# Prompt attention of a two-layer decoder step: scores from split operands in place of a plain f32 product

## The chip, the cores and the metric

The kernel runs on one core of a Trainium2 chip, in one launch. The metric is device time in microseconds, the median of three runs. The core has a matrix engine (TensorE, PE in the rows; its weight loads are PEld), a vector engine (VectorE, DVE), a scalar engine (ScalarE, ACT), GpSimd (POOL) and SyncE (SP), which here only issues transfers. ScalarE issues transfers too.

## The reference, cut to what matters

One inference step of a decoder of two layers: a Conformer convolution layer, then a layer of forgetting attention, each followed by a SwiGLU feed-forward. A prompt of 1024 tokens and eight sample requests of four tokens each go through it together. D is 1024, with 16 heads of 64. In the attention layer, for the prompt:

```python
p = xn @ w_in                     # q, k, v and the forget gate in one projection
logf = log_sigmoid(p[..., 3*D:] + b_f)
c = cumsum(logf, axis=1)
s = einsum('bqhd,bkhd->bhqk', qi, k) * dh**-0.5
s = s + ci[:, :, :, None] - cT[:, :, None, :]
s = where(kpos[None, :] <= qpos[:, None], s, -inf)
pr = softmax(s, axis=-1)
o = einsum('bhqk,bkhd->bqhd', pr, v)
```

Keys, values and logf of the prompt and of the samples are outputs as well. The samples attend to a paged cache of 1024 past rows each. All inputs and outputs are f32.

## The kernel before, in words

Activations are kept with features on the 128 partitions and the 1056 tokens (1024 prompt, 32 sample) along the free dimension, in three blocks of 352 columns. All large products are made of three passes over rounded operands (fp32r): each operand is split into a rounded part and the difference, as in xhi and xlo, whi and wlo, and `unit_block` (L693 to L709) adds up hi by hi, lo by hi and hi by lo. A unit is one chunk of 128 output features: three blocks by eight chunks by three passes, 72 matmuls. Weights are loaded by SP two units ahead, rounded by ScalarE (`hi_part`, L1133), and the difference is taken by GpSimd (`low_parts`, L618). Each engine has its own program; semaphores are the only order between them, and each engine and each transfer queue works in the order in which it is written.

In the attention layer the projection runs over pairs of units q: four pairs of queries (from Q_ATTN_IN), then the forget gate (L843 to L856), four pairs of keys (from QK), and four pairs of values (from QV). For queries and keys VectorE moves each block from PSUM to the staging tile stg, with one slot for each half s of a pair (`qk_half`, L1678), and ScalarE stores the 1024 prompt columns of it to q_scr or k_scr in device memory (`store_staged`, L1286). Keys and values are also transposed to token rows on TensorE (`keys_tr`, L858) and moved out by ScalarE (`keys_out`, `values_out`). The negated sums of logf, negct, are stored to c_scr (L1362). The sums for the sample requests are made by TensorE from the cached logf (L922 to L929), copied by VectorE to cbT (L1750) and stored by ScalarE to cb_scr (L1373).

Then comes the prompt attention, with heads in pairs. SP loads a head's queries, keys and its row of negated sums into one of two slots s of qa and ka (`load_head`, L505); the sums are the 65th row of ka, and the 65th row of qa is set to ones (L1756), so that one f32 product of 65 rows gives the scores with the sums of the keys. (The sum of the query's row falls out of the softmax.) A slot is loaded again when the last scores from it are through. Each head has eight query tiles of 128 rows, in the order 3, 2, 1, 0, 7, 6, 5, 4; tile qt has (qt + 1) * 128 key columns, done in pieces of up to 512. For tile t (`prompt_pair`, L978, L1383, L1777): TensorE makes the scores; VectorE adds the mask on the diagonal block (L1784) and takes the maximum (L1786); ScalarE makes the exponents and their sum (L1394); TensorE transposes them (`probs_tr`, L943); ScalarE copies them to pt (L1381); TensorE multiplies by the values (`values`, L952); VectorE divides (`output`, L1760). On TensorE the scores of tile t stand before the transposes of tile t-1 and the values of tile t-2; on ScalarE the copy of t-1 stands before the exponents of t.

After that come the eight sample requests, whose key pages SP loads into four buffers (`load_k`, L519). The first four pages are issued while the prompt attention runs (L543), the others after its last values (L546).

## Time and profile before

| | us |
|---|---|
| runs | 3438.42, 3446.14, 3453.70 |
| median | 3446.14 |
| span of the profiled execution | 3441.0 |
| TensorE busy | 2972.1 (86%) |
| VectorE busy | 1332.7 (39%) |
| ScalarE busy | 994.2 (29%) |
| GpSimd busy | 971.2 (28%) |

For the profiled execution the profile gives the span, from its first to its last instruction; its own time with what lies around the span is not listed apart from the runs. Matmuls are pipelined, so that their records overlap and a record is longer than the step from one start to the next; a plain f32 matmul shows as two weight loads and two matmuls. The granted clock of TensorE (PEclk) has two levels, 1.00 for 2.4 GHz and 0.50 for 1.2 GHz; a figure between them is a mean over a stretch. A wait is shown with the engine and the line that ended it; "issue" means that nothing in the profile ended it.

The projection of queries, keys and values takes the span from about 1500 to 1812 us, the prompt attention from 1824 to 2213, the sample requests from there to about 2500.

### The profile page before, as it was taken

The numbers are of one execution on the slowest core, as the hardware profiler recorded it, in microseconds if no ns is written. First come the engines' busy times: TensorE is split into PE (matmuls) and PEld (weight loads), VectorE is DVE, ScalarE is ACT, GpSimd is POOL, SyncE is SP. The second block draws the span as 40 slices with busy tenths as digits, with TensorE's granted clock in tenths as the row PEclk, the third lists the DMA queues.
The fourth block names the chain that finished last, engine by engine and source line by source line (L and its number), as shares of the span: only waits on it lengthen the run. The fifth ranks groups of instructions, "written<-read, shape, count | busy, mean of one in ns | idle before, by whom it ended". The sixth has DMA issues, their size and how long they took to land.

```text
span 3441.0 us, 49665 instructions
## 1 busy us (share of the span) xinstructions
PE 2972.1 (86%) x17970; PEld 2775.7 (81%) x17970; DVE 1332.7 (39%) x2005; ACT 994.2 (29%) x1549; POOL 971.2 (28%) x436
## 2 busy tenths in 40 slices
PE   5535336999999999989999999899898999999998
PEld 4535335889999999979997777778797999999997
DVE  6999996421111111251113555555334111111114
ACT  4323225232111111221113544455423211111113
POOL 2757571222212121231110000055613122222221
PEclk9767667999999999999996999988789999999998
DMA  3000000111111111122411201377511111111111
GB/s 95 19 24 12 24 12 20 43 37 40 52 40 46 43 43 49 37 68 82 121 39 31 70 25 25 101 254 262 195 43 37 40 46 43 40 52 34 52 36 70
DMA packets 243747, 206.54 MB, mean 60 GB/s; under 512 B 18252, under 2 KB 218956, under 8 KB 243652
## 3 DMA queue, kind: packets, MB, share of 16 engines
q1 hardware_dynamic: 230535, 186.66, 17.8%
q10 hardware_dynamic: 13133, 18.80, 1.6%
q8 instruction: 52, 0.85, 0.1%
q14 instruction: 27, 0.22, 0.0%
HBM read 183.16 MB, written 23.13 MB: 60 GB/s over the span
## 4 chain that ended last, share of the span: by engine, by line
PE 72%; DVE 15%; issue 7%; ACT 3%; DMA 1%; POOL 1%; DVEq 0%; ACTq 0%; SPq 0%; POOLq 0%
PE PS L706 19%; PE PS L708 18%; PE PS L707 18%; DVE yacc L1644 8%; PE PS L964 4%; PE PS L990 3%; PE PS L948 2%; DVE tm L1506 2%; PE PS L1027 1%; DVE rs L1485 1%; PE PS L1068 1%; PE PS L1040 1%; PE PS L1069 1%; PE PS L1041 1%; ACT pr L1394 1%
## 5 line engine op out<-in xcount | busy, mean ns | idle before, releaser
L706 PE MATMUL PS<-xhi,whi 128*128 128x352 f32 x3456 | 1144.4, 331 | 269.0 <-DVE u L1608 188.3
L708 PE MATMUL PS<-xlo,whi 128*128 128x352 f32 x3456 | 1122.3, 325 | 0.0
L707 PE MATMUL PS<-xhi,wlo 128*128 128x352 f32 x3456 | 1121.0, 324 | 0.0
L622 POOL TENSOR_TENSOR wlo<-wraw,whi 128x1024 fp32r<-128x1024 f32 x208 | 510.7, 2456 | 1608.4 <-ACT whi L1136 1608.4
L706 PEld LDWEIGHTS PS<-xhi,whi 128*128 128x128 f32 x3456 | 657.5, 190 | 311.6 <-DVE u L1608 190.3
L707 PEld LDWEIGHTS PS<-xhi,wlo 128*128 128x128 f32 x3456 | 660.9, 191 | 0.0
L708 PEld LDWEIGHTS PS<-xlo,whi 128*128 128x128 f32 x3456 | 658.6, 191 | 0.0
L1543 DVE TENSOR_TENSOR ht<-PS,ht 128x352 f32<-128x352 f32 x132 | 69.1, 525 | 908.4 <-PE PS L708 904.4
L1136 ACT ACTIVATE whi<-wraw 128x1024 fp32r<-128x1024 f32 x208 | 218.8, 1052 | 595.2 <-PE PS L708 567.2
L706 PE MATMUL PS<-hhi,whi 128*128 128x352 f32 x1056 | 341.2, 323 | 8.8 <-issue 8.8
L707 PE MATMUL PS<-hhi,wlo 128*128 128x352 f32 x1056 | 338.5, 321 | 0.0
L708 PE MATMUL PS<-hlo,whi 128*128 128x352 f32 x1056 | 338.2, 320 | 0.0
L1644 DVE SCALAR_TENSOR_TENSOR yacc<-u,wc,yacc 128x1024 f32<-128x1024 f32 x152 | 329.5, 2168 | 3.7
L679 POOL TENSOR_TENSOR Vl<-vr,Vh 128x1024 fp32r<-128x1024 f32 x64 | 151.7, 2383 | 531.6 <-ACT Vh L1420 531.6
L1529 DVE TENSOR_TENSOR X<-PS,X 128x352 f32 x216 | 113.3, 525 | 446.8 <-PE PS L708 446.4
L644 POOL TENSOR_TENSOR yp<-yp,prods 128x1024 f32<-128x1024 f32 x72 | 217.0, 3013 | 10.3
L706 PEld LDWEIGHTS PS<-hhi,whi 128*128 128x128 f32 x1056 | 198.1, 188 | 10.8 <-issue 10.8
L707 PEld LDWEIGHTS PS<-hhi,wlo 128*128 128x128 f32 x1056 | 198.4, 188 | 0.0
L708 PEld LDWEIGHTS PS<-hlo,whi 128*128 128x128 f32 x1056 | 197.9, 187 | 0.0
L1241 ACT ACTIVATE prods<-u,wc 128x1024 f32<-128x1024 f32 x88 | 98.7, 1148 | 298.7 <-DVE u L1613 199.3
L1191 ACT ACTIVATE hhi<-ht 128x352 f32 x132 | 65.5, 498 | 410.6 <-DVE ht L1543 410.6
L990 PE MATMUL PS<-ka,qa 65*128 65x512 f32 (+3 forms) x384 | 165.6, 544 | 3.6 <-issue 3.6
(197 smaller groups left out, 3036.5 us busy)
## 6 DMA issues: line engine op xcount, KB each, us to landing
wraw<-in_ffn_w_gu SPq DMA_DIRECT2D x88, 512.0 KB, 3.8
kr<-in_cache_k SPq DMA_DIRECT2D x64, 512.0 KB, 4.8
vr<-in_cache_v SPq DMA_DIRECT2D x64, 512.0 KB, 4.8
wraw<-in_ffn_w_down SPq DMA_DIRECT2D x32, 384.0 KB, 3.4
wraw<-in_attn_w_in SPq DMA_DIRECT2D x24, 512.0 KB, 3.9
wraw<-in_ffn_w_down SPq DMA_DIRECT2D x32, 320.0 KB, 3.1
wraw<-in_conv_w_in SPq DMA_DIRECT2D x16, 512.0 KB, 3.8
wraw<-in_conv_w_out SPq DMA_DIRECT2D x8, 512.0 KB, 4.0
```

The source lines that it names most:

```text
L622: nc.gpsimd.tensor_tensor(wlo[:, s, :], wraw[:, s, :], whi[:, s, :].bitcast(F32), ALU.subtract).then_inc(w_lo, 1)
L644: nc.gpsimd.tensor_tensor(yp[:, :], prods[:, 0, :] if i == 1 else yp[:, :], prods[:, i % 3, :], ALU.add).then_inc(p_tap, 1)
L679: nc.gpsimd.tensor_tensor(Vl[:, j % 2, :], raw_values(j), Vh[:, j % 2, :].bitcast(F32), ALU.subtract).then_inc(v_lo, 1)
L706: nc.tensor.matmul(out, wh, hi[:, k, blk(b)], start=(k == 0), stop=False)
L707: nc.tensor.matmul(out, wl, hi[:, k, blk(b)], start=False, stop=False)
L708: m = nc.tensor.matmul(out, wh, lo[:, k, blk(b)], start=False, stop=(k == kc - 1))
L964: m = nc.tensor.matmul(PS[:, 6 + t % 2, 0:DH], pt[:, t % 2, kb * P:(kb + 1) * P], v, start=(kb == 0), stop=(kb == nb - 1))
L990: m = nc.tensor.matmul(PS[:, 2 * (t % 2) + k0 // 512, 0:k1 - k0], qa[:, s, qt * P:(qt + 1) * P], ka[:, s, k0:k1], start=True, stop=True)
L1136: nc.scalar.activation(whi[:, s, :], wraw[:, s, :], ACT.Copy).then_inc(w_hi, 1)
L1241: nc.scalar.activation(prods[:, i % 3, :], u[:, k:k + SEQ], ACT.Copy, scale=wc[:, R_DW + k:R_DW + k + 1]).then_inc(a_tap, 1)
L1529: nc.vector.tensor_tensor(xs, PS[:, NB * s + b, 0:BW], xs, ALU.add).then_inc(ev[s], 1)
L1644: step(nc.vector.scalar_tensor_tensor(yacc[:, :], u[:, k:k + SEQ], wc[:, R_DW + k:R_DW + k + 1], yacc[:, :], ALU.mult, ALU.add))
```

## The change

Queries and keys are split into a rounded part (hi) and the difference (lo) right after the projection: ScalarE copies each staged block to shi, rounded; VectorE subtracts it into slo; ScalarE stores both, to two scratch tensors each. The negated sums are split in the same way (chi, clo). A head now loads q1 = (q hi over q hi) and k1 = (k hi over k lo), each of 128 rows, and q2 = (q lo and two rows of ones) and k2 = (k hi and the two rows of the sums), each of 66 rows. The scores are two matmuls on rounded operands that add up in PSUM: q1 by k1, and q2 by k2. The product of the two lo parts is left out.

The new tiles lie where others lay: shi and slo in the place of Vt (values), q2 in the place of cbT, pt in the place of ktok, two of the buffers of the key pages. From this come new waits: SP loads heads after cbT has been stored, VectorE sets the ones after that too, values are written after the last stores of queries and keys, and key pages 2 and 3 of the first request are loaded after the last values of the prompt.

```diff
--- before.py
+++ after.py
@@ -190,10 +190,19 @@
         lc = at("lc", [P, NPG, NREQ, H], F32, where["sq"][0])
         cbT = at("cbT", [NREQ * H, NPG * P], F32, where["rs"][0])
 
-        qa = at("qa", [DH + 1, 2, SEQ], F32, where["xhi"][0])
-        ka = at("ka", [DH + 1, 2, SEQ], F32, after("qa"))
-        pr = at("pr", [P, 2, SEQ], F32, after("ka"))
-        pt = at("pt", [P, 2, SEQ], F32, after("pr"))
+        shi = at("shi", [P, 2, SEQ], FR, where["Vt"][0])
+        slo = at("slo", [P, 2, SEQ], FR, after("shi"))
+        chi = at("chi", [H, SEQ], FR, where["rs"][0])
+        clo = at("clo", [H, SEQ], FR, where["ssq"][0])
+
+        q1 = at("q1", [P, 2, SEQ], FR, where["xhi"][0])
+        k1 = at("k1", [P, 2, SEQ], FR, after("q1"))
+        k2 = at("k2", [DH + 2, 2, SEQ], FR, after("k1"))
+        pr = at("pr", [P, 2, SEQ], F32, after("k2"))
+        assert after("pr") <= where["xlo"][0]
+        q2 = at("q2", [DH + 2, 2, SEQ], FR, where["rs"][0])
+        assert after("q2") <= where["tm"][0]
+        pt = at("pt", [P, 2, SEQ], F32, where["ktok"][0])
         on = at("on", [P, NT, P], F32, where["tm"][0])
         OT = at("OT", [P, C, T], F32, where["xlo"][0])
 
@@ -224,9 +233,9 @@
         yn = at("yn", [P, C, T], F32, where["xhi"][0])
         ytok = at("ytok", [P, 2, D], F32, H0)
 
-        q_scr = nc.dram_tensor("q_scr", (D, SEQ), F32).ap()
-        k_scr = nc.dram_tensor("k_scr", (D, SEQ), F32).ap()
-        c_scr = nc.dram_tensor("c_scr", (H, SEQ), F32).ap()
+        q_scr = [nc.dram_tensor(f"q_scr{part}", (D, SEQ), F32).ap() for part in ("hi", "lo")]
+        k_scr = [nc.dram_tensor(f"k_scr{part}", (D, SEQ), F32).ap() for part in ("hi", "lo")]
+        c_scr = nc.dram_tensor("c_scr", (2, H, SEQ), F32).ap()
         cb_scr = nc.dram_tensor("cb_scr", (NREQ * H, NPG * P), F32).ap()
 
         PS = ctx.enter_context(nc.psum_tensor("PS", [P, 8, 512], F32))
@@ -290,6 +299,10 @@
         c_neg = sem("c_neg")
         c_tr = sem("c_tr")
         c_nc = sem("c_nc")
+        c_hi = sem("c_hi")
+        c_lo = sem("c_lo")
+        st_hi = sem("st_hi")
+        st_lo = sem("st_lo")
         c_st = sem("c_st")
         lc_ld = sem("lc_ld")
         x_mm = sem("x_mm")
@@ -499,14 +512,23 @@
             for s in range(2):
                 sp.wait_ge(mm[s], Q_ATTN_OUT * NB)
             for s in range(2):
-                sp.wait_ge(stg_st[s], 16 * C)
-            sp.wait_ge(c_st, 16)
+                sp.wait_ge(stg_st[s], 32 * C)
+            sp.wait_ge(c_st, 32)
+
+            sp.wait_ge(x_ev, 2)
+            sp.wait_ge(cb_st, 16)
 
             def load_head(i, s):
                 h = i * 2 + s
-                sp.dma_start(qa[0:DH, s, :], q_scr[ds(h * DH, DH), :]).then_inc(a_ld[s], 16)
-                sp.dma_start(ka[0:DH, s, :], k_scr[ds(h * DH, DH), :]).then_inc(a_ld[s], 16)
-                sp.dma_start(ka[DH:DH + 1, s, :], c_scr[ds(h, 1), :]).then_inc(a_ld[s], 16)
+                rows = ds(h * DH, DH)
+                sp.dma_start(q1[0:DH, s, :].bitcast(F32), q_scr[0][rows, :]).then_inc(a_ld[s], 16)
+                sp.dma_start(k1[0:DH, s, :].bitcast(F32), k_scr[0][rows, :]).then_inc(a_ld[s], 16)
+                sp.dma_start(q1[DH:P, s, :].bitcast(F32), q_scr[0][rows, :]).then_inc(a_ld[s], 16)
+                sp.dma_start(k1[DH:P, s, :].bitcast(F32), k_scr[1][rows, :]).then_inc(a_ld[s], 16)
+                sp.dma_start(q2[0:DH, s, :].bitcast(F32), q_scr[1][rows, :]).then_inc(a_ld[s], 16)
+                sp.dma_start(k2[0:DH, s, :].bitcast(F32), k_scr[0][rows, :]).then_inc(a_ld[s], 16)
+                sp.dma_start(k2[DH:DH + 2, s, :].bitcast(F32), c_scr[:, ds(h, 1), :].rearrange("a h t -> a (h t)")
+                             ).then_inc(a_ld[s], 16)
             load_head(0, 0)
             load_head(0, 1)
             with sp.Fori(1, C) as i:
@@ -540,14 +562,13 @@
 
             for s in range(2):
                 sp.wait_ge(kt_st[s], 16 * C // 2)
-            for j in range(4):
+            for j in range(2):
                 load_k(0, j)
 
             sp.wait_ge(a_pv, NTILES)
             sp.wait_ge(w_lo, 2 * Q_ATTN_OUT + 2)
-            sp.wait_ge(cb_st, 16)
             load_sums(0)
-            for j in range(4, NPG):
+            for j in range(2, NPG):
                 load_k(0, j)
 
             def load_step(b):
@@ -981,15 +1002,16 @@
                 for t in range(NTAU):
                     s, qt = t // NT, ORDER[t % NT]
                     if t % NT == 0:
-                        pe.wait_ge(a_ld[s], i * 48 + 48)
+                        pe.wait_ge(a_ld[s], i * 112 + 112)
 
                     past(pe, a_exp, base + (t - 1))
                     nk = (qt + 1) * P
-                    for k0 in range(0, nk, 512):
-                        k1 = min(nk, k0 + 512)
-                        m = nc.tensor.matmul(PS[:, 2 * (t % 2) + k0 // 512, 0:k1 - k0],
-                                             qa[:, s, qt * P:(qt + 1) * P], ka[:, s, k0:k1],
-                                             start=True, stop=True)
+                    for e0 in range(0, nk, 512):
+                        e1 = min(nk, e0 + 512)
+                        out = PS[:, 2 * (t % 2) + e0 // 512, 0:e1 - e0]
+                        nc.tensor.matmul(out, q1[:, s, qt * P:(qt + 1) * P], k1[:, s, e0:e1], start=True, stop=False)
+                        m = nc.tensor.matmul(out, q2[:, s, qt * P:(qt + 1) * P], k2[:, s, e0:e1],
+                                             start=False, stop=True)
                     m.then_inc(a_sc, 1)
                     if t >= 1:
                         probs_tr(base, t - 1)
@@ -1285,10 +1307,18 @@
 
             def store_staged(q, s, scr, q0):
 
-                act.wait_ge(ev[s], seen(s, q, NB - 1))
-                act.nop(nofuse=True)
-                act.dma_start(scr[ds(q * (2 * P) + (s * P - q0 * 2 * P), P), :], stg[:, s, 0:SEQ]
-                              ).then_inc(stg_st[s], 16)
+                past(act, stg_st[s], (q - Q_ATTN_IN) * 32)
+                for b in range(NB):
+                    act.wait_ge(ev[s], seen(s, q, b))
+                    act.nop(nofuse=True)
+                    cols = slice(b * BW, min((b + 1) * BW, SEQ))
+                    nc.scalar.activation(shi[:, s, cols], stg[:, s, cols], ACT.Copy).then_inc(st_hi, 1)
+                act.wait_ge(st_hi, (q - Q_ATTN_IN) * (2 * NB) + (s * NB + NB))
+                act.wait_ge(st_lo, (q - Q_ATTN_IN) * (2 * NB) + (s * NB + NB))
+                for part, split in zip(scr, (shi, slo)):
+                    act.nop(nofuse=True)
+                    act.dma_start(part[ds(q * (2 * P) + (s * P - q0 * 2 * P), P), :], split[:, s, :].bitcast(F32)
+                                  ).then_inc(stg_st[s], 16)
 
             with act.Fori(Q_ATTN_IN, QK) as q:
                 for s in range(2):
@@ -1359,14 +1389,21 @@
             next_hi(QV, 0)
             next_hi(QV, 1)
             act.wait_ge(c_nc, 2)
-            act.dma_start(c_scr, negct[:, :]).then_inc(c_st, 16)
+            nc.scalar.activation(chi[:, :], negct[:, :], ACT.Copy).then_inc(c_hi, 1)
+            for s in range(2):
+                act.wait_ge(stg_st[s], 32 * C)
             values_out(QV, 0)
+            act.wait_ge(c_hi, 1)
+            act.wait_ge(c_lo, 1)
+            act.dma_start(c_scr[0], chi[:, :].bitcast(F32)).then_inc(c_st, 16)
+            act.dma_start(c_scr[1], clo[:, :].bitcast(F32)).then_inc(c_st, 16)
             with act.Fori(QV + 1, Q_ATTN_OUT) as q:
                 next_hi(q, 0)
                 values_out(q - 1, 1)
                 next_hi(q, 1)
                 values_out(q, 0)
             values_out(Q_ATTN_OUT - 1, 1)
+            act.wait_ge(c_st, 32)
             new_out(vnew, 2)
             act.wait_ge(kt_ev, 4 * C)
             act.wait_ge(x_ev, 2)
@@ -1393,6 +1430,8 @@
                     past(act, a_tr, base + (t - 1))
                     nc.scalar.activation(pr[:, t % 2, 0:nk], banks(2 * (t % 2), nk), ACT.Exp,
                                          bias=nmx[:, t:t + 1], accum_out=den[:, t:t + 1]).then_inc(a_exp, 1)
+            for s in range(2):
+                act.wait_ge(kt_st[s], 16 * C // 2)
             prompt_pair(0)
             act.dma_start(v_prompt[0, 0].rearrange("(t p) h d -> p t (h d)", p=P), Vt[:, :, :]).then_inc(v_st, 16)
             act.dma_start(v_sample[0].rearrange("b t h d -> (b t) (h d)"), vnew[:, :]).then_inc(v_st, 16)
@@ -1679,10 +1718,6 @@
 
                 u = (q - Q_ATTN_IN) * 2 + s
 
-                if values:
-                    dve.wait_ge(stg_st[s], 16 * C)
-                else:
-                    past(dve, stg_st[s], (q - Q_ATTN_IN) * 16)
                 if keys:
                     past(dve, kt_tr, ((q - QK) * 2 + (s - 1)) * 2)
                 for b in range(NB):
@@ -1693,6 +1728,11 @@
                             PS[:, NB * s + b, BW - NS:BW], scale, None, ALU.mult).then_inc(nqk, 1)
                     nc.vector.tensor_scalar(stg[:, s, blk(b)], PS[:, NB * s + b, 0:BW], scale, None,
                                             ALU.mult).then_inc(ev[s], 1)
+                for b in range(0 if values else NB):
+                    dve.wait_ge(st_hi, u * NB + (b + 1))
+                    cols = slice(b * BW, min((b + 1) * BW, SEQ))
+                    nc.vector.tensor_tensor(slo[:, s, cols], stg[:, s, cols], shi[:, s, cols].bitcast(F32),
+                                            ALU.subtract).then_inc(st_lo, 1)
 
             def qk_pair(q, scale, keys, values=False):
                 for s in range(2):
@@ -1743,9 +1783,13 @@
                 dve.wait_ge(c_tr, half + 1)
                 nc.vector.tensor_copy(negct[:, 512 * half:512 * half + 512], PS[0:H, 6 + half, :]
                                       ).then_inc(c_nc, 1)
+            dve.wait_ge(c_nc, 2)
+            dve.wait_ge(c_hi, 1)
+            nc.vector.tensor_tensor(clo[:, :], negct[:, :], chi[:, :].bitcast(F32), ALU.subtract).then_inc(c_lo, 1)
             with dve.Fori(QV + 1, Q_ATTN_OUT) as q:
                 qk_pair(q, 1.0, True, True)
             dve.wait_ge(x_mm, 1)
+            dve.wait_ge(c_st, 32)
             for half in range(2):
                 nc.vector.tensor_copy(cbT[:, 512 * half:512 * half + 512], PS[:, 6 + half, :]).then_inc(x_ev, 1)
             dve.wait_ge(nm_tr, 1)
@@ -1753,7 +1797,8 @@
                                   ).then_inc(x_ev, 1)
 
 
-            nc.vector.memset(qa[DH:DH + 1, :, :], 1.0).then_inc(a_ones, 1)
+            dve.wait_ge(cb_st, 16)
+            nc.vector.memset(q2[DH:DH + 2, :, :].bitcast(F32), 1.0).then_inc(a_ones, 1)
 
             dve.wait_ge(out_st, 16 * 3)
```

## Rows read from the trace of the kernel before

**Rows 1.** The page: its first line and the chain's shares by line.

```profile
span 3441.0 us, 49665 instructions
...
PE PS L706 19%; PE PS L708 18%; PE PS L707 18%; DVE yacc L1644 8%; PE PS L964 4%; PE PS L990 3%; PE PS L948 2%; DVE tm L1506 2%; PE PS L1027 1%; DVE rs L1485 1%; PE PS L1068 1%; PE PS L1040 1%; PE PS L1069 1%; PE PS L1041 1%; ACT pr L1394 1%
```

**Rows 2.** Chain that ended last, attention stretch: start us, us, engine and line.

```profile
1835.39 3.52 PE PS L990 x4
...
1873.79 3.52 PE PS L990 x4
...
2012.28 1.79 PE PS L990 x4
...
2057.26 1.79 PE PS L990 x4
```

**Rows 3.** Timeline of one head: start us, us, engine, line, operation [idle before].

```profile
2012.60 0.19 PEld L990 LDWEIGHTS PS<-ka,qa 65*128 65x128 f32 x1 [0.24 <-issue]
...
2013.03 0.19 PEld L990 LDWEIGHTS PS<-ka,qa 65*128 65x128 f32 x1 [0.24 <-issue]
...
2016.94 1.09 PE L948 MATMUL PS<-ident,pr 128*128 128x128 f32 x8 [0.82 <-ACT pr L1394]
...
2020.14 0.98 PE L948 MATMUL PS<-ident,pr 128*128 128x128 f32 x7 [0.59 <-ACT pr L1394]
```

**Rows 4.** Waits of TensorE, 1824 to 2213: total us, times, longest.

```profile
PE PS L948 <- ACT pr L1394: 21.1, 31, 0.8
```

**Rows 5.** Timeline of TensorE, sample stage, rounded operands of 512 columns.

```profile
2299.81 0.39 PE L1068 MATMUL PS<-Vh,PTs 128*128 128x512 f32 x1
2300.04 0.39 PE L1069 MATMUL PS<-Vl,PTs 128*128 128x512 f32 x1
```

**Rows 6.** Groups by line: count, busy us, mean ns, idle before.

```profile
L1147 ACT ACTIVATE xhi<-tm 128x352 fp32r<-128x352 f32 x96 | 47.8, 498 | 78.6 <-DVE tm L1506 78.6
```

**Rows 7.** Timelines of ScalarE and TensorE at the forget gate.

```profile
1584.05 1.06 ACT L1136 ACTIVATE whi<-wraw 128x1024 fp32r<-128x1024 f32 x1 [10.30 <-PE PS L708]
...
1587.73 0.66 PE L847 MATMUL PS<-xhi,wfs 128*128 128x352 f32 x1 [3.71 <-DVE wfs L1707]
```

**Rows 8.** Timeline of TensorE at the end of the keys.

```profile
1702.75 1.03 PE L887 MATMUL PS<-ident,newqk 128*32 128x128 f32 x8 [1.49 <-ACT ktok L1316]
```

**Rows 9.** Timelines at the start and the end of prompt attention.

```profile
1821.79 0.36 ACTq L1373 DMA_DIRECT2D cb_scr<-cbT  x1
...
1824.35 3.32 PE L990 MATMUL PS<-ka,qa 65*128 65x512 f32 x4 [3.62 <-issue]
...
2210.96 0.63 SPq L536 DMA_DIRECT2D cbx<-cb_scr  x1
```

**Rows 10.** DMA issues: size and us from issue to landing.

```profile
cb_scr<-cbT ACTq DMA_DIRECT2D x1, 512.0 KB, 2.6
```

**Rows 11.** DMA queues, 1806 to 1830: packets, MB, share of that time.

```profile
q1 hardware_dynamic: 324, 1.06, 20.4%
```

**Rows 12.** Windows: length, busy us of PE, PEld, DVE, ACT, POOL, then PEclk.

```profile
1824.00:1884.00 60.00, 58.53 (x187) 42.96 (x188) 19.97 (x53) 17.10 (x39) 0.00 (x0) 0.50 0.04 9
1885.00:2208.00 323.00, 299.90 (x1969) 234.19 (x1968) 178.03 (x470) 162.33 (x345) 0.00 (x0) 1.00 0.14 41
...
2126.50:2130.00 3.50, 2.75 (x11) 1.27 (x9) 2.56 (x6) 1.46 (x3) 0.00 (x0) 1.00 0.00 0
2208.50:2212.00 3.50, 2.05 (x17) 1.62 (x15) 1.39 (x5) 0.00 (x0) 0.00 (x0) 1.00 0.00 0
...
2213.60:2220.40 6.80, 6.04 (x29) 5.53 (x28) 3.14 (x3) 3.69 (x4) 0.00 (x0) 0.50 0.44 125
...
2273.50:2276.50 3.00, 3.00 (x19) 2.47 (x18) 2.29 (x4) 2.75 (x4) 2.13 (x1) 0.50 0.34 132
2277.00:2280.00 3.00, 2.37 (x17) 1.96 (x16) 2.14 (x5) 1.97 (x2) 2.07 (x1) 1.00 0.35 108
```

**Rows 13.** Timeline of TensorE, 2270 to 2278.

```profile
2275.45 1.75 PE L1027 MATMUL PS<-ident,kr 128*128 128x128 f32 x8
```

## The prediction

> **What bounds the kernel now.** I read the page's chain of waits first, then the attention stretch by its chain in order of time, its timeline and its waits, then windows for the clock. The chain runs through the projection and feed-forward matmuls (L706 to L708), which the diff leaves alone; of what it touches, L990 (scores) holds 3% of a 3441.0 us span, L964 4%, L948 2% [rows 1]. The prompt attention is 16 heads of 8 query tiles. In its steady part two heads take 44.98 us (2012.28 to 2057.26) [rows 2], 22.5 a head.
>
> Inside a head TensorE does, per tile, scores, the transposes of the tile before and the values of the one before that. A plain f32 score matmul of 512 columns is two records, 0.43 us apart by the starts of their weight loads [rows 3], so 0.86. Tiles are 512, 384, 256, 128, 1024, 896, 768 and 640 columns wide: 4608 columns, nine times 512, 7.7 us a head. But TensorE is not the bound at every tile: before the transposes of the 1024 and the 896 tile it stands for 0.82 and 0.59 us until ScalarE's exponent is through [rows 3], and over the stage such waits come to 21.1 us [rows 4]. From one of these transposes to the next is 3.2 us (2016.94 to 2020.14), a ring of transposes, ScalarE's copy, its exponent and again transposes, with no score matmul in it.
>
> **The matmuls.** Rounded operands of 512 columns start 0.23 us apart [rows 5]; two passes make 0.46 instead of 0.86. Nine such: 4.1 instead of 7.7, 3.6 less a head, 58 over 16. How much arrives, tile by tile (0.78 us per 1000 columns): the 1024 tile saves 0.80, and since the long wait behind it starts at its end, all of it counts. The 896 tile lies inside that wait, the 768 tile beside the 3.2 us ring: nothing, the waits grow by 0.70 and 0.60. The 640, 512, 384, 256 and 128 tiles save 0.50, 0.40, 0.30, 0.20 and 0.10, 1.5 together, where the trace shows TensorE itself late; ScalarE's ring comes next there, and I take 1.1. So 1.9 a head, 30 us. The bounds are 0.8 (13 us) and 3.6 (58 us) a head. That 128 columns go as fast, each, as 512 is not shown; if the two 128 wide pieces of a head gained nothing, 0.2 a head, 3 us, would go. Contraction rows (128 and 66 for 65) are not in the time of a matmul; I cost them at nothing.
>
> **Splitting at the projection.** 16 units of queries and keys each gain three ScalarE copies (0.5 us each, as the same shape takes in L1147 [rows 6]), three VectorE differences of about that, and a second store. ScalarE stands 10.30 us before its next piece of a unit [rows 7], which hides these 2.4 us (with the last difference and the second issue); VectorE no longer waits for the store of the unit. Without that cover it would be 16 times 2.4, 38 us. It shows at two places where TensorE already waits for these engines. At the forget gate it waits 3.71 us for VectorE's wfs [rows 7], which waits for a ScalarE copy now queued behind three copies, the last difference and one more issue: 1.5 + 0.5 + 0.4, 2.4, and 3 with some of it at the low clock (2 to 5). At the end of the keys it waits 1.49 us for ScalarE's ktok [rows 8], behind the same three things: 2.4 again, I take 3 (2 to 5). The split of the sums c lies beside four pairs of value projections, nobody waits for it before the loads: nothing.
>
> **The start of attention.** In the kernel before, SP issues the loads of the first two heads ahead of time, beside the last projection work. The change makes SP wait until cbT is stored, because q2 lies in its place; behind that wait on SP stand all head loads. The store is issued at 1821.79 [rows 9] and lands 2.6 us later [rows 10], 1824.4. A head is now six transfers of 256 KB and one of 8, 1.58 MB instead of 0.52. Two heads' old loads, 1.06 MB, took 20.4% of 24 us [rows 11], 4.9 us or 216 GB/s; so 7.3 us, plus 1.4 for the first issue and the wake-up (an estimate, half of the 2.6): scores start near 1833.1 and not at 1824.35 [rows 9]. That is 9 us. The bounds are 5, at twice that rate, and 16.5, with both heads' 3.2 MB mixed. VectorE's memset of the ones (now two rows) waits for the same store and lies beside the loads. Later loads, 7.3 us a head in 20, hide; nothing else is on SP's queue then.
>
> **The end of attention.** pt takes the place of two page buffers, so key pages 2 and 3 of the first request are loaded after the last values, behind SP's load of the sums at 2210.96 [rows 9]; TensorE has pages 0 and 1 to transpose first: 1.5 us (0 to 3, as a transfer of that size lands in 2.6 [rows 10]).
>
> **The clock.** From 1824 to 1884 the granted clock was 0.50, the level of 1.2 GHz, after TensorE had stood for 3.62 us [rows 9, 12]; a head cost 38.4 us there (1835.39 to 1873.79) [rows 2] instead of 22.5. With the change a head there saves nine times 0.80, some 7 us, less a little for waits: 32. But the full clock is nearer its end later on. It held over 2126.5 to 2130.0 with TensorE busy 2.75 of 3.50 us, and was 0.50 after 2208.5 to 2212.0, busy 2.05 of 3.50 [rows 12]; halving the scores of the first of these stretches takes 0.7 us out of it. I expect a low stretch at the start about as long as now, cheaper by some 7, and about one new fall inside the stage, dearer by about the same: 0. Bounds: 20 less (no low stretch), or 140 more (all heads low).
> The Trainium skill ("TensorE: Matmul & The Clock Gate", PE-mode transpose) says that transposes don't engage the full clock. By that rule the change takes away half of what holds it, and the all-low rival below would be the time. The trace speaks against it: 2273.5 to 2276.5 was at 0.50 with transposes on TensorE, and 2277 to 2280 is at 1.00 [rows 12, 13].
> The same page (Why this matters for your kernels) asks for no idle gaps over about 3 us; by that rule the grown waits, at most 1.5 us, would cost no clock at all. No run here shows it yet: the fall behind 2208.5 came with 1.45 us idle in all.
>
> **Sum.** Against the profiled execution (span 3441.0): -30 + 9 + 3 + 3 + 1.5 + 0 = -13.5. The median of the runs, 3446.14, lies 5.1 above that span; 13 off it gives 3433.
>
> **Rivals.**
> Scores alone set the pace: TensorE's 58 us arrive, or the low stretch at the start goes (20): 41 or 33 less, 3405 to 3413. For it, TensorE is busy 299.90 of 323 us of the stage [rows 12]; against it, the waits on ScalarE of [rows 3, 4].
> Costs eat the gain: of the five smaller tiles nothing arrives (13 us for 30), or less than half of it while the loads of two heads mix (16.5 for 9) and the two projection waits run to 5: 3446 to 3461. For it, ScalarE's ring, which already ends some tiles; against it, that these five show no wait as long as at the two wide ones [rows 3].
> The low clock comes back in attention, the one that ends slower: place, the waits before the transposes of the 1024 and 896 tiles, now 1.5 and 1.2 us; price, 32 less 20.6, 11.4 us a head at 1.2 GHz. It decides from about 1.2 heads more than now (gain gone); from 2.7 heads more, the result is slower by over 0.5%. All 16 low: 16 times 32 is 512 instead of 387 (1824.35 to 2210.96) [rows 9], plus 16.5 of other costs, on the median: 3588. For it, the two stretches above; against it, the full clock from 1885 to 2208 [rows 12] in spite of the same two waits in every head.
> The change doesn't do what it says: a rounded pass on 128 rows takes as long as an f32 record (0.43); then no gain and 16.5 more, 3463. Against it, [rows 5].
>
> **Chances.** Forecast 0.50 (own range 3420 to 3448), pace 0.17, costs 0.15, clock 0.13, no speed-up 0.05. A measurement of this kernel can tell about 0.5%, 17 us, from no change. Faster than 3429: the pace and two fifths of the forecast, 0.37; slower than 3463: clock, most of the no speed-up, 0.18; same 0.45. The range 3406 to 3468 leaves out the all-low end of the clock and the best of the pace, under 0.2.
>
> **What would show it.** In the profile after: pairs of score records 0.23 apart at 512 columns; a head near 20.6; waits before the 1024 and 896 transposes of about 1.5 and 1.2; first scores 9 us later behind the cbT store; L847 and the new-key transposes 2 to 3 later behind ScalarE. I am wrong if heads take under 19.5 or over 22, if windows inside attention after the first two heads show a clock well under 1.00 for long, or if the first scores start within 6 us of the old place.

## The result, and the profile after

The changed kernel took 3474.58 us (median of four runs, 3459.56 to 3480.02) where the kernel before took 3449.44 beside it (3438.42 to 3453.70): ratio 1.0079, interval 1.0049 to 1.0110. That is slower by 0.8%, where 3433 and a gain of 0.4% were forecast, and above the range of 3406 to 3468. Here and below the ratios rest on the runs in the faster of the core's two states, so they are not the quotients of the medians, which are over all runs. The profiled execution took 3459.56 us and is the fastest of the four; its span, 3457.8, is 16.8 us longer than the 3441.0 of [rows 1].

The page of the changed kernel: span, granted clock in 40 slices, the chain's shares by line. L1012 and L1013 are the two score passes, L969 the transposes, L985 the values.

```profile
span 3457.8 us, 50031 instructions
...
PEclk9767667999999999999996798989789999999999
...
PE PS L727 19%; PE PS L729 18%; PE PS L728 18%; DVE yacc L1683 8%; PE PS L985 4%; PE PS L969 2%; DVE tm L1545 2%; PE PS L1049 1%; DVE rs L1524 1%; PE PS L1090 1%; PE PS L1012 1%; PE PS L1091 1%; PE PS L1062 1%; PE PS L1063 1%; PE PS L1013 1%
```

Scores fell from 3% of the chain to about 2%, as meant; the time went elsewhere. Three marks cut the span, here from the timelines of ScalarE's, SP's and TensorE's queues in the changed kernel (start us, us, what [idle before]):

```profile
1830.45 0.36 ACTq L1410 DMA_DIRECT2D cb_scr<-cbT  x1
...
1833.14 0.56 SPq L524 DMA_DIRECT2D q<-q_scrhi  x1
...
1843.10 0.77 PE L1012 MATMUL PS<-k,q 128*128 128x512 f32 x1 [13.70 <-DMA k<-c_scr]
...
2230.91 0.65 SPq L558 DMA_DIRECT2D cbx<-cb_scr  x1
```

Against [rows 9] the store of cbT is 8.7 us later (the projection), the first scores 18.75 later (so 10.1 more at the start of attention). From first scores to the load of the sums it is 387.8 us where it was 386.6: the stage that should have lost 30 us lost nothing. What follows it is 3.1 shorter.

The pace of the heads was as forecast. Starts of the 16 value matmuls of the 1024 tile, from the chain in order of time:

```profile
1865.09 3.31 PE PS L985 x16
1897.31 3.31 PE PS L985 x16
...
2002.20 1.73 PE PS L985 x16
2023.67 1.73 PE PS L985 x16
2043.51 1.73 PE PS L985 x16
```

Two heads take 41.31 us from 2002.20, 20.65 each (forecast 20.6); at the start one takes 32.2 (forecast 32). One head from TensorE's timeline, the counterpart of [rows 3], and the waits from 1843 to 2213, the counterpart of [rows 4] (up to the stage's end at 2230.9 they come to 37.5 us in 35 waits):

```profile
2015.74 0.40 PE L1013 MATMUL PS<-k,q 66*128 66x512 f32 x1
2015.98 0.40 PE L1012 MATMUL PS<-k,q 128*128 128x512 f32 x1
...
2019.49 1.10 PE L969 MATMUL PS<-ident,pr 128*128 128x128 f32 x8 [1.50 <-ACT pr L1431]
...
2022.69 0.98 PE L969 MATMUL PS<-ident,pr 128*128 128x128 f32 x7 [1.17 <-ACT pr L1431]
```

```profile
PE PS L969 <- ACT pr L1431: 34.7, 32, 2.7
```

The passes start 0.24 apart and the two waits grew to 1.50 and 1.17, where 1.5 and 1.2 were forecast. What was not foreseen stands in the windows (length, busy us of PE, PEld, DVE, ACT, POOL, then PEclk):

```profile
1833.20:1918.40 85.20, 70.31 (x294) 64.80 (x295) 29.06 (x74) 26.42 (x57) 0.00 (x0) 0.50 0.43 124
1918.50:1966.20 47.70, 39.77 (x302) 35.64 (x301) 29.32 (x77) 24.96 (x54) 0.00 (x0) 1.00 0.31 70
1966.30:2000.30 34.00, 33.27 (x141) 30.81 (x139) 12.34 (x34) 12.25 (x26) 0.00 (x0) 0.50 0.21 47
2000.40:2102.70 102.30, 87.77 (x677) 79.63 (x677) 61.49 (x164) 55.42 (x119) 0.00 (x0) 1.00 0.34 77
2102.80:2136.80 34.00, 33.27 (x141) 30.81 (x140) 12.34 (x34) 12.15 (x26) 0.00 (x0) 0.50 0.20 47
2136.90:2230.90 94.00, 80.44 (x625) 73.19 (x623) 53.40 (x143) 50.23 (x105) 0.00 (x0) 1.00 0.26 62
```

153.2 us ran at 1.2 GHz (0.50) in three stretches. The first began while TensorE still waited for the loads, so 143.3 us of them lie after the first scores; the kernel before had one stretch of about 60 there [rows 12]. An estimate from the heads' own times: at 32 us a head, 143.3 us are 4.5 heads that cost 11.4 more each, 51; the stretch before was 1.6 heads of 38.4 that cost 15.9 more each, 25. The difference, 26, is most of the 30 us that the shorter score work saved.

### The profile page after: what moved, and what is told of

It is laid out like the page before. It is cut to its first block, busy times and chain, and to the rows that moved or that the text cites. A ratio compares the mean times of both kernels' runs of the same rounds, so it can differ in the third digit from the quotient of the medians.

```text
span 3457.8 us, 50031 instructions
## 1 busy us (share of the span) xinstructions
PE 2958.0 (86%) x17970; PEld 2813.3 (81%) x17970; DVE 1368.2 (40%) x2054; ACT 1014.3 (29%) x1598; POOL 972.1 (28%) x436
## 4 chain that ended last, share of the span: by engine, by line
PE 71%; DVE 15%; issue 8%; ACT 3%; DMA 1%; POOL 1%; DVEq 0%; SPq 0%; ACTq 0%; POOLq 0%
PE PS L727 19%; PE PS L729 18%; PE PS L728 18%; DVE yacc L1683 8%; PE PS L985 4%; PE PS L969 2%; DVE tm L1545 2%; PE PS L1049 1%; DVE rs L1524 1%; PE PS L1090 1%; PE PS L1012 1%; PE PS L1091 1%; PE PS L1062 1%; PE PS L1063 1%; PE PS L1013 1%
## 5 line engine op out<-in xcount | busy, mean ns | idle before, releaser
L727 PE MATMUL PS<-hhi,whi 128*128 128x352 f32 x1056 | 341.2, 323 | 8.8 <-issue 8.8
L985 PEld LDWEIGHTS PS<-Vt,pt 128*128 128x128 f32 x1152 | 170.7, 229 | 9.9 <-DVE OT L1819 7.0
```

The lines of the kernel that those rows point to most:

```text
L727: nc.tensor.matmul(out, wh, hi[:, k, blk(b)], start=(k == 0), stop=False)
L985: m = nc.tensor.matmul(PS[:, 6 + t % 2, 0:DH], pt[:, t % 2, kb * P:(kb + 1) * P], v, start=(kb == 0), stop=(kb == nb - 1))
```

## The experiments

Two theories. The clock: the gain arrives at 2.4 GHz and is given back because TensorE, with half of its score work gone and longer waits, loses the full clock. The rival: the loads, the splitting or ScalarE hold the stage, and the clock only shows it. The fences of code are cuts of the edits; lines left out are marked. Each ratio is to the kernel before on the same chip; the series ran on three chips.

**Extra work in the waits.** TensorE gets matmuls whose results nobody reads: in the wait ahead of the first scores (second kernel), in the two waits of each head (third), in both (first).

```diff
+            for _ in range(14):
+                nc.tensor.matmul(PS[:, 5, :], Vt[:, 0, 0:P], Vt[:, 0, 0:512], start=True, stop=True)
             pe.wait_ge(a_ones, 1)
...
                     m.then_inc(a_sc, 1)
+                    fill = {7: 5, 6: 4}.get(ORDER[(t - 1) % NT], 0)
+                    if fill:
+                        past(pe, a_pt, base + t - 1)
+                    for _ in range(fill):
+                        nc.tensor.matmul(PS[:, 5, :], q1[:, s, 0:P], k1[:, s, 0:512], start=True, stop=True)
```

> The changed kernel with extra TensorE work whose results nobody reads: 14 plain f32 matmuls of 512 columns (about 12 us) in the 13.7 us in which TensorE waits for the first head's loads, and in every head 5 and 4 rounded matmuls of 512 columns (1.17 and 0.94 us at 0.23) in the waits of 1.50 and 1.17 us ahead of the transposes of the 1024 and 896 tiles. Theory (the 1.2 GHz clock took the gain back): the changed kernel has 153 us at 0.50 in attention, 4.8 heads that cost 32 us instead of 20.6, 11.4 each; with the clock held, 54 us come back: about 3421, attention from first scores to the load of the sums about 335 us instead of 388, no stretch of 0.50 in it. Rival (the clock falls because the stage waits for something else, loads or ScalarE, and costs nothing by itself): the waits are still there, extra work in them changes nothing, 3475, or a little more.

> The changed kernel with the 14 extra matmuls ahead of the first scores only. Theory: the 85 us at 0.50 that begin in that wait go (2.6 heads of 11.4, 30 us), falls of the clock inside the stage (two of 34 us) stay: about 3445. Rival (the low clock at the start follows from the narrow first tiles or costs nothing): the first scores start at the same place, the stretch is there, 3470 to 3477.

> The changed kernel with the extra matmuls in the two waits of each head only. Theory: the two falls inside attention (68 us at 0.50, 2.1 heads of 11.4, 24 us) go, and the low stretch at the start ends sooner, as the extra work also raises what TensorE does at the low clock (0 to 20 us): 3430 to 3451. Rival (the waits have no part in the falls; the rounded score passes by themselves hold the clock worse): falls stay, and at 0.50, where the waits are shorter, the extra work costs up to 2 us a head: 3475 to 3490.

Measured: both 3410.75 (3407.01 to 3414.64), steps alone 3413.73 (3411.39 to 3414.79), start alone 3468.81 (3438.47 to 3501.18). Ratios to the kernel before: 0.9854 (0.9794 to 0.9914), 0.9857 (0.9798 to 0.9916), 1.0004 (0.9966 to 1.0042). With the steps filled, the start and the end of the stage, its windows and the wait at the 1024 tile:

```profile
1843.83 0.77 PE L1012 MATMUL PS<-k,q 128*128 128x512 f32 x1 [13.87 <-DMA k<-c_scr]
...
2185.03 0.66 SPq L558 DMA_DIRECT2D cbx<-cb_scr  x1
```

```profile
1843.90:1862.90 19.00, 15.46 (x56) 13.19 (x57) 7.17 (x18) 6.38 (x15) 0.00 (x0) 0.50 0.30 64
1863.00:2185.00 322.00, 308.23 (x2262) 274.85 (x2260) 187.96 (x507) 175.59 (x370) 0.00 (x0) 1.00 0.35 86
```

```profile
2025.87 1.30 PE L1020 MATMUL PS<-k,q 128*128 128x512 f32 x5
2027.54 1.09 PE L969 MATMUL PS<-ident,pr 128*128 128x128 f32 x8 [0.37 <-ACT pr L1436]
```

More work, less time: the full clock holds for 322 us on end, and the stage (1843.83 to the load of the sums at 2185.03) takes 341.2 us instead of 387.8. That is 46.6 of the 51 that the low clock was reckoned to cost, and 19 us at 1.2 GHz are left (7 us by the same price). Both kernels with the steps filled came out below what was expected (about 3421; 3430 to 3451); with the steps alone the first low stretch shrank from 75 us behind the first scores to 19. The rival falls: loads, splitting and ScalarE's work are as they were. Work at the start alone only put the first fall off; windows of that kernel:

```profile
1831.30:1846.70 15.40, 13.31 (x32) 5.87 (x32) 3.52 (x5) 1.19 (x1) 0.00 (x0) 1.00 0.87 203
1846.90:1894.60 47.70, 45.09 (x185) 41.13 (x186) 17.75 (x48) 17.23 (x40) 0.00 (x0) 0.50 0.21 45
1894.70:1997.00 102.30, 87.71 (x678) 79.62 (x677) 61.46 (x164) 55.46 (x119) 0.00 (x0) 1.00 0.44 120
1997.10:2055.00 57.90, 56.78 (x246) 53.43 (x245) 20.11 (x55) 19.99 (x42) 0.00 (x0) 0.50 0.25 55
```

With a third stretch of 34 us that is 139.6 us at 1.2 GHz, where the changed kernel had 143.3 behind its first scores. The expected 30 us did not come. The first low stretch lasted 47.7 us with the start filled and 19 with the steps filled, so in these profiles it is the waits inside the heads, not the one ahead of them, that keep the clock low for long.

**The kernel before with extra work**, first only ahead of its first scores, then (a kernel by itself) in the two waits of each head:

```diff
+            for _ in range(4):
+                nc.tensor.matmul(PS[:, 5, :], Vt[:, 0, 0:P], Vt[:, 0, 0:512], start=True, stop=True)
             pe.wait_ge(a_ones, 1)
...
                     m.then_inc(a_sc, 1)
+                    fill = {7: 384, 6: 320}.get(ORDER[(t - 1) % NT], 0)
+                    if fill:
+                        past(pe, a_pt, base + t - 1)
+                        nc.tensor.matmul(PS[:, 5, 0:fill], Vt[:, 0, 0:P], Vt[:, 0, 0:fill], start=True, stop=True)
```

> The kernel before with four extra f32 matmuls of 512 columns (3.4 us) in its wait of 3.62 us ahead of the first scores. Control: if the low stretch at the start (61 us at 0.50) comes from that wait and costs about 11 us a head, 61 us are 1.6 heads of 38.4 instead of 22.5, so 25 us come back: 3424. If the extra work only helps because of something in the change: 3449.

> The kernel before with one extra plain f32 matmul of 384 columns (0.65 us) ahead of the transposes of the 1024 tile and one of 320 (0.54) ahead of those of the 896 tile, in its waits of 0.82 and 0.59. Theory (the clock, in both kernels): its runs come together at the lower end and below it, 3420 to 3440, and the difference to the changed kernel with the same cure (3414) is what the change is worth at equal clock: forecast 13. Rival (only the changed kernel loses the clock): 3450 to 3475, as the kernel before.

Measured: start 3468.82, ratio 1.0003 (0.9962 to 1.0045), a miss like the one above; steps 3424.89 (3423.98 to 3427.98), ratio 0.9891 (0.9832 to 0.9950). Timelines and windows of the latter:

```profile
1822.05 3.33 PE L990 MATMUL PS<-ka,qa 65*128 65x512 f32 x4 [3.62 <-issue]
...
2193.74 0.63 SPq L536 DMA_DIRECT2D cbx<-cb_scr  x1
```

```profile
1821.10:1845.00 23.90, 21.83 (x58) 13.93 (x59) 8.63 (x21) 6.47 (x17) 0.00 (x0) 0.50 0.02 9
1845.00:2193.70 348.70, 341.15 (x2179) 263.83 (x2178) 190.81 (x505) 173.95 (x369) 0.00 (x0) 1.00 0.13 40
```

So the kernel before loses the clock too: with its waits filled it is faster, and its runs lie within 4 us. The change can now be weighed with the clock held in both but for some 20 us at the start: the stage of the kernel before takes 371.7 us (1822.05 to 2193.74), the changed one's 341.2, 30.5 less, with 30 forecast. Priced as above, the 23 us at 1.2 GHz here and the 19 there account for about 3 of these 30.5. As wholes, on two chips, 3424.89 and 3413.73 are 11.2 apart, with 13.5 forecast.

**The changed kernel again**, unaltered:

> The changed kernel once more, unaltered, beside many more runs of the kernel before, which lay between 3441 and 3482 in the last series (median 3474) where the first four lay between 3438 and 3454. Theory (both kernels hold the full clock only by a little, so that each run has its own share of the stage at 1.2 GHz): no step between the two, ratio 0.99 to 1.005, and each of them spreads over 30 us or more. Rival (the change makes it slower by itself): the ratio 1.008 stands.

Measured: 3461.52 (3449.70 to 3503.02), ratio 1.0005 (0.9960 to 1.0049) to a kernel before with a median of 3475.15 there. The profile of this repeat has the low stretches of the first one again (85, 34 and 34 us) and a stage of 387.8 us. The 0.8% of the first comparison did not come back: its four runs of the kernel before were from the lower part of a wide spread. In the runs of the kernel before on this chip, 3438.58 goes with a mean granted clock of 0.925 and 3475.15 with 0.913. By (1 - clock) x time / 0.5 that is about 89 us more at 1.2 GHz, and at 15.9 of 38.4 us (the price worked out above) 37 us, for 36.6 measured. This is an estimate from one pair of runs, and it takes the low clock to lie in attention; only spans and mean clocks of these runs are kept, not where the clock fell.

**Is it being busy that holds the clock?** As the third kernel, but each extra matmul contracts one row:

```diff
-                        nc.tensor.matmul(PS[:, 5, :], q1[:, s, 0:P], k1[:, s, 0:512], start=True, stop=True)
+                        nc.tensor.matmul(PS[:, 5, :], q1[0:1, s, 0:P], k1[0:1, s, 0:512], start=True, stop=True)
```

> As the changed kernel with the 5 and 4 extra matmuls in the waits (3414), but each extra matmul contracts 1 row where it contracted 128: the same columns and, in the records, the same time. If an instruction on TensorE is enough to hold the clock: 3410 to 3418. If it goes by what the array does, not by whether an instruction runs: as without extra work, 3455 to 3480, with stretches of 0.50 in attention.

Measured: 3501.41 (3458.28 to 3502.98), ratio 1.0085 (1.0040 to 1.0130). From its timeline, then its windows:

```profile
2016.98 1.42 PE L1020 MATMUL PS<-k,q 1*128 1x512 f32 x5
```

```profile
1937.80:2060.60 122.80, 119.16 (x860) 103.86 (x861) 72.92 (x196) 66.05 (x143) 0.00 (x0) 1.00 0.34 78
2060.70:2118.60 57.90, 57.90 (x235) 52.10 (x233) 18.50 (x49) 17.98 (x37) 0.00 (x0) 0.50 0.25 55
```

One row takes about as long as 128 (1.42 for five, against 1.30), TensorE counts as busy for 119.16 of 122.80 us, and the clock falls all the same. The extra instructions and their waits are those of the third kernel, so it was not their place that made that one faster. The time is longer than without extra work, and longer than either theory said: the stage takes 427.4 us (1842.17 to 2269.57), about 210 of them at 1.2 GHz. Why the low stretches grew is not shown.

**Loads early.** Extra work in the steps, and q2 in the place of the raw weights, so that SP need not wait for cbT (VectorE's ones and the load of the sums change their waits to match):

```diff
-        q2 = at("q2", [DH + 2, 2, SEQ], FR, where["rs"][0])
+        q2 = at("q2", [DH + 2, 2, SEQ], FR, where["wraw"][0])
...
-            sp.wait_ge(x_ev, 2)
-            sp.wait_ge(cb_st, 16)
+            sp.wait_ge(w_lo, 2 * Q_ATTN_OUT + 2)
```

> The changed kernel with the extra matmuls in the waits, and q2 laid in the place of the raw weights, which are free when the last low part is made (about 1819), so that SP issues the heads' loads there and not behind the store of cbT (1833). Forecast's term for the later start was 9 us, the trace after shows about 10: first scores some 10 us earlier (near 1833 where the profile has 1843), 3403 to 3406. Rival (the transfers then collide with the stores and the cb matmuls, or the clock's low stretch grows as much): 3412 to 3416.

Measured: 3403.69 (3401.75 to 3405.11), ratio 0.9825 (0.9766 to 0.9883). Its first scores:

```profile
1832.98 0.77 PE L1011 MATMUL PS<-k,q 128*128 128x512 f32 x1 [3.62 <-issue]
```

10.9 us earlier than the 1843.83 of the third kernel, and the time is 10.0 less than its 3413.73, on another chip. That bears out the start term.

**The splitting put in another order.** On top of that, the forget gate's weights are split ahead of the last query pair, and the last keys' and new keys' copies go ahead of the last unit's rounding (ScalarE's part; VectorE's follows it):

```diff
-            with act.Fori(Q_ATTN_IN, QK) as q:
+            with act.Fori(Q_ATTN_IN, QK - 1) as q:
                 for s in range(2):
                     next_hi(q, s)
                     store_staged(q, s, q_scr, Q_ATTN_IN)
             act.wait_ge(f_ld, 48)
             nc.scalar.activation(wfs[:, :, 0:H], wfr[:, :, :], ACT.Copy).then_inc(f_hi, 1)
+            for s in range(2):
+                next_hi(QK - 1, s)
+                store_staged(QK - 1, s, q_scr, Q_ATTN_IN)
...
+            keys_out(QV - 1, 1)
             new_out(kns, 0)
+            store_staged(QV - 1, 1, k_scr, QK)
```

> The kernel with extra matmuls in the waits and early head loads (3404), and the splitting put out of the way at the two places where TensorE waits: ScalarE's and VectorE's parts of the forget gate's weights ahead of the last query pair, and at the end of the keys ScalarE's copies for the last keys and the new keys ahead of the rounding copies of the last unit. Forecast's terms were 3 and 3; the trace after shows the stage's end 8.7 us later. If all of that is these two queues: about 3395. If it is spread over the 16 units: 3401 to 3405.

Measured: 3388.15 (3387.14 to 3390.73), ratio 0.9810 (0.9762 to 0.9858): 15.5 less than the kernel with early loads, on another chip, and more than the 8.7. TensorE at the two places, of the changed kernel and then of this one (with its first scores), with their windows (1560 to 1600, 1680 to 1720):

```profile
1590.10 0.66 PE L868 MATMUL PS<-xhi,wfs 128*128 128x352 f32 x1 [6.63 <-DVE wfs L1747]
...
1707.97 1.86 PE L908 MATMUL PS<-ident,newqk 128*32 128x128 f32 x8 [3.96 <-ACT ktok L1346]
```

```profile
1560.00:1600.00 40.00, 33.37 (x198) 33.09 (x197) 15.77 (x24) 6.89 (x13) 8.86 (x9) 0.91 0.24 92
1680.00:1720.00 40.00, 35.19 (x208) 33.88 (x208) 8.58 (x20) 9.32 (x18) 4.76 (x2) 0.87 0.56 174
```

```profile
1693.67 1.03 PE L907 MATMUL PS<-ident,newqk 128*32 128x128 f32 x8 [0.89 <-ACT ktok L1353]
...
1815.34 0.77 PE L1011 MATMUL PS<-k,q 128*128 128x512 f32 x1 [3.62 <-issue]
```

```profile
1560.00:1600.00 40.00, 40.00 (x252) 40.00 (x251) 16.93 (x25) 6.54 (x13) 8.90 (x9) 1.00 0.26 94
1680.00:1720.00 40.00, 37.71 (x249) 36.62 (x248) 8.15 (x18) 7.73 (x14) 5.97 (x3) 1.00 0.45 137
```

The wait for wfs is gone, also the 3.71 that the kernel before already had; that for ktok is 0.89, below the 1.49 of the kernel before [rows 7, 8]. With them goes the low clock in both windows, by their means of 0.91 and 0.87 about 18 us at 1.2 GHz. The first scores start 17.6 us before the 1832.98 of the kernel with early loads.

**One pass.** Extra work in the steps, the second score pass left out:

```diff
-                        nc.tensor.matmul(out, q1[...], k1[...], start=True, stop=False)
-                        m = nc.tensor.matmul(out, q2[...], k2[...], start=False, stop=True)
+                        m = nc.tensor.matmul(out, q1[...], k1[...], start=True, stop=True)
```

> The changed kernel with the extra matmuls in the waits (3414), the second score pass (q2 with k2) left out: the sums and a low part are missing from the scores. It takes another nine times 0.23, 2.1 us a head, off TensorE. If what arrives is about half, as the forecast has it for the change's own 3.6 (1.9): 16 off, 3398. If scores set the pace: 33 off, 3381. If ScalarE ends the tiles by now: 3412 to 3414.

Measured: 3395.16 (3393.66 to 3396.68), 18.6 less than the third kernel's 3413.73 on another chip; its stage takes 322.8 us (1841.20 to 2164.01), 18.4 less. That is about half of the 33 taken off TensorE, as the forecast had it.

**The order of the tiles**, without any extra work; then with early loads and the mended queues:

```diff
-        ORDER = [3, 2, 1, 0, 7, 6, 5, 4]
+        ORDER = [3, 2, 1, 0, 4, 5, 6, 7]
```

> The changed kernel with no extra work, but each head's tiles in the order 512, 384, 256, 128, 640, 768, 896, 1024 columns, so that no 1024 wide tile follows the 128 wide one with nothing to do for TensorE behind it. If the waits of 1.50 and 1.17 us come from that order and with them the falls of the clock: waits under 1 us, a head under 20.6, no long stretch at 0.50 behind the first head, 3405 to 3425. Rival (the waits only move to other tiles, and the rounded scores hold the clock no better): 3455 to 3480.

> Early head loads, mended queues at the projection and the order of tiles 512, 384, 256, 128, 640, 768, 896, 1024, no extra work. If the order alone holds the clock: 3385 to 3405. If not: about 19 less than the changed kernel, 3440 to 3460.

Measured: 3408.32 (3400.82 to 3420.21), ratio 0.9875 (0.9826 to 0.9925); all together 3382.68 (3379.61 to 3386.28), ratio 0.9794 (0.9745 to 0.9842), some 2% under the kernel before on the same chip. The changed kernel with the order alone, its waits from 1845 to 2150 and windows:

```profile
PE PS L969 <- ACT pr L1431: 26.5, 44, 0.9
```

```profile
1839.30:1859.10 19.80, 16.25 (x64) 14.32 (x65) 8.49 (x22) 7.94 (x19) 0.00 (x0) 0.50 0.29 62
1859.20:2169.70 310.50, 276.50 (x2109) 245.93 (x2108) 186.71 (x503) 174.13 (x367) 0.00 (x0) 1.00 0.36 89
```

Waits in more and smaller parts, none above 0.9 us, and the clock holds for 310 us although TensorE is busy for 276.50 of them only. The stage takes 330.5 us (1839.31 to 2169.79), 10.7 less than with the steps filled: no extra work lies in the way, and over the whole stage these waits come to 31.5 us, where the changed kernel had 37.5. What each of the two gives was not taken apart. The order was not tried in the kernel before. How much of the 2% is due to the change, and how much the order would have given without it, stays open.

## Why the prediction was wrong

- **The clock: the step that failed.** The prediction had "a low stretch at the start about as long as now" and "about one new fall", worth 0. It was 85 us at the start (75 behind the first scores) and two falls of 34, worth about 26 by the prices of a head. The 20.6 and the 32 us a head were right; how many heads run at which was not. The prediction's own sign, a clock well under 1.00 for long inside attention, came true. I had named the rival, its place and its price, and gave it 0.13: the full clock from 1885 to 2208 [rows 12] was read as room to spare, from one execution. The repeats, with mean clocks down to 0.912, and the gain from filling its waits show that the kernel before often loses the clock too; the one profile was a good execution.
- **The base.** The sum was hung on one profiled execution and a median of three runs. Over the 20 runs on one chip on which its ratio rests, that kernel reaches from 3437 to 3484. A difference of 13 us was to be read from a quantity that wanders by 47. Beside more runs of it the change makes no difference that can be told (1.0005, 0.9960 to 1.0049); what the first comparison's 0.8% holds beyond the choice of runs was not settled.
- **The matmuls: right.** 20.65 a head, waits 1.50 and 1.17, stage 30.5 less at held clock for 30.
- **Splitting at the projection: place right, size 8.7 for 6.** The wait for wfs grew by 2.9 and that for ktok by 2.5, as forecast. Two things were not counted. At the end of the keys TensorE then ran at 1.2 GHz for some 10 us (from 1706.8), busy for 9.03 of 10.10 us; the kernel before held 1.00 there. And the 352-column differences, costed at 0.5 us, took 1.1 in the mean, which mixes two sizes. In each of the eight query units the first of the three differences took 2.38 to 2.45 us; it ran beside GpSimd's difference for the weights, which had begun just before and took as long. The other two took about 0.5 each. At the forget gate the first is 1.9 us longer than costed, ahead of wfs. No experiment took GpSimd's work away, so that the one lengthens the other is only argued. The window, the group of VectorE's differences by line (count, busy us, mean ns, idle before) and the last query unit's:

```profile
1706.90:1717.00 10.10, 9.03 (x38) 8.22 (x39) 0.88 (x2) 2.26 (x4) 0.00 (x0) 0.50 0.67 215
```

```profile
L1734 DVE TENSOR_TENSOR slo<-stg,shi 128x352 fp32r<-128x352 f32 x30 | 32.4, 1117 | 25.4 <-ACT shi L1315 25.4
...
1584.64 2.34 POOL L643 TENSOR_TENSOR wlo<-wraw,whi 128x1024 fp32r<-128x1024 f32 x1 [8.94 <-ACT whi L1158]
1584.98 3.22 DVE L1734 TENSOR_TENSOR slo<-stg,shi 128x352 fp32r<-128x352 f32 x3 [0.73 <-ACT shi L1315]
```

- **The start of attention: right.** 10.1 for 9, the first scores 10.0 us behind SP's first issue; without SP's wait for cbT 10 us came back.
- **The end of attention: 1.5 costed, none seen.** What follows the load of the sums is not longer but 3.1 us shorter, which no experiment took apart. So the costs came out close in sum (8.7 + 10.1 - 3.1, 15.7 for 16.5) in part by luck: one that did not come made up for one that was too small.

## What to carry to other kernels

Before work is taken off TensorE in a stage that holds 2.4 GHz with waits in it, reckon the new stage at both levels of the clock, and look at the granted clock of several executions, not of one. Where the clock is in doubt, try to spread the waits rather than count on them to be free: here another order of the tiles held the clock without extra work. Extra matmuls into which all 128 rows enter held it too; with one row they did not. Then price the change with the clock held in both kernels: only so was it seen here that the stage itself had become 30.5 us shorter, for 30 forecast.

## What the runs showed of the hardware

- The granted clock fell at 1966 and 2102.8 although TensorE had stood for no longer than 1.51 us at a time in the full-clock stretches before (from 1918.5 and 2000.4). The Trainium skill ("TensorE: Matmul & The Clock Gate", Why this matters for your kernels) asks for no gap over about 3 us; the measurement differs: here keeping to that was not enough.
- One row and 128 rows take about the same time on TensorE, 1.42 and 1.30 us for five matmuls of 512 columns. The same page and section of the Trainium skill says so of 32 rows; here one row, which it does not name, comes within 0.12 us. For the clock they are not the same: 322 us at 1.00 with 128 rows, a fall to 0.50 after 122.8 us with one, TensorE busy for 97% of them.
